# Layer boundaries of an fp32 two-block transformer kernel run in token halves, with scaled tiles in PSUM

## What is computed

```python
    y = jnp.concatenate([y_fox, y_dsa, y_mem], axis=-1)
    y = jnp.einsum('bsn,nd->bsd', y, w_out)
    return layer_norm(ALPHA * x + y, ln_gain, ln_bias)
...
    h = jnp.einsum('bsd,dn->bsn', x, w_in)          # next layer, on the normalised rows
...
    a = rms_norm(h, g_mix_pre[l])                   # second block, on those of layer 2
    proj = a @ w_in[l]
```

## Time and profile before

| | us |
|---|---|
| median of 3 runs | 2196.77 (2196.4 to 2198.25) |
| profiled execution, as a run | 2198.66 |
| its span, first to last instruction | 2196.8 |
| TensorE matmuls busy | 2158.5 |
| VectorE / ScalarE / GpSimd busy | 1279.6 / 1101.5 / 401.4 |

### The profile page before, as it was taken

One profiled execution on the slowest core, in us unless ns is written; L12 is line 12 of the kernel. 1 busy time (PEld: TensorE's weight loads), 2 busy tenths in 40 slices (PEclk: granted clock), 3 DMA queues, 4 the chain that ended last, 5 costly groups with the idle time before them and its releaser, 6 DMA issues.

```text
span 2196.8 us, 29512 instructions
## 1 busy us (share of the span) xinstructions
PE 2158.5 (98%) x11798; PEld 1866.0 (85%) x11798; DVE 1279.6 (58%) x1858; ACT 1101.5 (50%) x1526; POOL 401.4 (18%) x176
## 2 busy tenths in 40 slices
PE   8999999999999999999999999999999999999998
PEld 7888888888988888888888888788888888888886
DVE  5544448765566437855577666665655555555556
ACT  4444554554364554545455455646534534544543
POOL 0000333431000334332006876000000000000000
PEclk9999999999999999999999999999999999999999
DMA  8666555655666555565656655545666666666664
GB/s 287 187 184 185 158 146 162 174 163 174 191 184 185 162 154 154 173 173 163 191 167 199 191 175 161 191 139 169 190 193 191 189 194 192 186 194 193 188 193 141
DMA packets 324376, 394.66 MB, mean 180 GB/s; under 512 B 20320, under 2 KB 252384, under 8 KB 323472
## 3 DMA queue, kind: packets, MB, share of 16 engines
...
## 4 chain that ended last, share of the span: by engine, by line
PE 90%; DVE 5%; ACT 3%; issue 2%; DMA 1%; SPq 0%; DVEq 0%; ACTq 0%
PE acc L645 32%; PE acc L660 17%; PE acc L662 12%; PE acc L647 12%; PE acc L648 12%; ACT high L870 1%; PE tb L711 1%; DVE low L477 1%; PE tb L587 1%; PE obank L733 1%; ACT sc L902 1%; PE sbank L757 1%; PE sbank L701 0%; ACT sc L913 0%; DVE yf L1236 0%
## 5 line engine op out<-in xcount | busy, mean ns | idle before, releaser
L870 ACT ACTIVATE high<-raw 128x1024 fp32r<-128x1024 f32 (+1 forms) x729 | 764.5, 1051 | 790.6 <-PE acc L660 199.4
L477 DVE TENSOR_TENSOR low<-raw,high 128x1024 fp32r<-128x1024 f32 (+1 forms) x569 | 710.7, 1250 | 634.0 <-ACT high L870 630.8
L645 PE MATMUL acc<-xhl,high 128*128 128x512 f32 x3200 | 779.9, 394 | 4.1 <-ACT cb L1159 2.2
L645 PEld LDWEIGHTS acc<-xhl,high 128*128 128x128 f32 x3200 | 586.6, 189 | 116.9 <-issue 2.8
L477 POOL TENSOR_TENSOR low<-raw,high 128x1024 fp32r<-128x1024 f32 x160 | 393.8, 2465 | 743.1 <-ACT high L870 743.0
L660 PE MATMUL acc<-xhl,low 128*128 128x256 f32 x3200 | 434.1, 286 | 2.7 <-DVE low L477 1.4
L660 PEld LDWEIGHTS acc<-xhl,low 128*128 128x128 f32 x3200 | 418.1, 192 | 21.1 <-DVE xhl L1654 1.7
L647 PE MATMUL acc<-high,yhl 128*128 128x512 f32 (+1 forms) x1044 | 384.1, 374 | 1.4 <-DVE work L1528 1.4
L648 PE MATMUL acc<-high,yhl 128*128 128x512 f32 (+1 forms) x1044 | 382.4, 373 | 0.0
L662 PE MATMUL acc<-low,yhl 128*128 128x512 f32 (+1 forms) x1044 | 243.3, 374 | 0.4 <-DVE yhl L1630 0.2
L647 PEld LDWEIGHTS acc<-high,yhl 128*128 128x128 f32 x1044 | 196.8, 188 | 35.9 <-DVE work L1528 1.8
...
## 6 DMA issues: line engine op xcount, KB each, us to landing
raw<-in_w_in SPq DMA_DIRECT2D x336, 512.0 KB, 3.7
raw<-in_w_ff SPq DMA_DIRECT2D x256, 512.0 KB, 4.2
raw<-in_w_out SPq DMA_DIRECT2D x91, 512.0 KB, 4.6
raw<-in_w_mem_kv SPq DMA_DIRECT2D x32, 512.0 KB, 4.9
...
x_nat<-in_mem SPq DMA_DIRECT2D x4, 512.0 KB, 7.7
x_nat<-in_x POOLq DMA_DIRECT2D x4, 512.0 KB, 6.7
yf<-in_ln_gain POOLq DMA_DIRECT2D x2, 1024.0 KB, 5.0
```

The lines of the kernel that those rows point to most:

```text
L477: eng.tensor_tensor(part(low, g), part(raw, g), part(high, g).bitcast(F32), ALU.subtract).then_inc(ready, 1)
L645: ins = pe.matmul(acc[:, 2 * (c.acc % 2) + s, :], wh[:, t, at], vhl, start=first, stop=last)
L870: act.activation(part(high, g), part(raw, g), ACT.Copy).then_inc(high_ready, 1)
```

## The change

- The output projection of the two layers has four chunks of 512 columns (`FCOLS`); statistics are taken over 512 columns per call.
- The last four blocks of its last chunk are done for token tile 0 first, then for tile 1 (`edge`). VectorE does residual, statistics, variance and small steps for each tile by itself (`last_residual`, `row_stats`, `row_var`, `row_scale`), and ScalarE one root for each.
- The first four units are normalised, transposed, scaled and split for tile 0 and then for tile 1; the first four blocks of the next projection run for tile 0 and then tile 1. Units 4 to 7 stay whole. The 36 filler matmuls go.
- The scaled tiles lie in the PSUM banks `sbank` and `obank` (`scaled`) and not in `cb`.
- The lows of the next projection's first eight blocks are GpSimd's. Its queue issues the two row transfers between the fourth and the fifth.
- VectorE's list: the second tile's residual comes behind the scaling of unit 1, its statistics and variance behind unit 1's low part, its small steps behind the scaling of unit 2.
- The rest of the diff renumbers semaphore targets.

```diff
-        for n, (col, width) in enumerate(COLS):
+        for n, (col, width) in enumerate(FCOLS):
...
-        stats = vec("stats", 96).rearrange("p (s c k) -> p s c k", s=ST, c=8)
+        stats = vec("stats", 48).rearrange("p (s c k) -> p s c k", s=ST, c=NF)
...
+        def tiles_in(phase, u, s=0):
+
+            return 12 * phase + (4 * s + u + 1 if u < 4 else 8 + u - 3)
+
+        def scaled(u):
+
+            if u >= 4:
+                return (sbank, obank)[u % 2][:, :].rearrange("p (h n) -> p h n", h=2)
+            return (sbank, obank)[u // 2][:, u % 2 * S:u % 2 * S + S].rearrange("p (h n) -> p h n", h=2)
+
+        edges = [(by[("o", l, NF - 1)].blocks[-4:], by[("fv", l + 1, 0) if l + 1 < DEPTH else ("v2", 0)].blocks)
+                 for l in range(DEPTH)]
...
-        pool_blocks = [[LAYER0 + LAYER_SLOTS * l + b for b in range(40, 134) if b % 2] for l in range(DEPTH)]
+        pool_blocks = [[LAYER0 + LAYER_SLOTS * l + b for b in range(40, 134) if b % 2] + edges[l][1]
+                       for l in range(DEPTH)]
...
+                elif k == ("fv", 0, 0):
+                    pe.wait_ge(xt_ready, 8 + first)
+                elif k == ("v2", 0) or k[0] == "fv" and k[2] == 0:
+                    pe.wait_ge(xt_ready, 16 + tiles_in(k[1] - 1 if k[0] == "fv" else 1, first - 1, rows[-1]))
...
-                if c.blocks.index(g) % 2:
+                if c.blocks.index(g) % 2 and rows != (0,):
                     with_low(False)
                     ins = with_high(False, g == c.blocks[-1])
                 else:
                     with_high(g == c.blocks[0], False)
+                    if between:
+                        between()
                     ins = with_low(g == c.blocks[-1])
...
+            def half_transposes(l, s, u):
+
+                pe.wait_ge(norm_ready, norms(l, u, s))
+                t = t_begin(("nT", l, u, s))
+                for dt in range(2):
+                    ins = pe.transpose(t[:, dt * S + s * P:dt * S + s * P + P],
+                                       x[:, s, 256 * u + dt * P:256 * u + dt * P + P], ident)
+                t_end(ins, ("nT", l, u, s))
+
+            def full_transposes(l, u):
+
+                pe.wait_ge(norm_ready, norms(l, u))
+                transpose_unit(("nT", l, u), x, 256 * u)
+
+            def edge(l):
+
+                out, into = edges[l]
+                for g in out:
+                    weight_block(g, (0,))
+                for g in out[:3]:
+                    weight_block(g, (1,))
+                half_transposes(l, 0, 0)
+                weight_block(out[3], (1,))
+                half_transposes(l, 0, 1)
+                weight_block(into[0], (0,))
+                half_transposes(l, 0, 2)
+                half_transposes(l, 0, 3)
+                weight_block(into[1], (0,))
+                weight_block(into[2], (0,))
+                weight_block(into[3], (0,), lambda: half_transposes(l, 1, 0))
+                half_transposes(l, 1, 1)
+                weight_block(into[0], (1,))
+                half_transposes(l, 1, 2)
+                half_transposes(l, 1, 3)
+                weight_block(into[1], (1,))
+                full_transposes(l, 4)
+                weight_block(into[2], (1,))
+                full_transposes(l, 5)
+                weight_block(into[3], (1,))
+                for u in range(4, 8):
+                    if u < 6:
+                        full_transposes(l, u + 2)
+                    weight_block(into[u])
...
-                    if l and b < 6:
-
-                        pe.wait_ge(norm_ready, norms(l - 1, b + 2))
-                        transpose_unit(("nT", l - 1, b + 2), x, 256 * (b + 2))
-                    weight_block(g0 + b)
+                    if (l == 0 or b >= 8) and b < LAYER_SLOTS - 4:
+                        weight_block(g0 + b)
...
-                spin(job_no(l, "dsa", HS - 1), 36)
-                for u in range(2):
-                    pe.wait_ge(norm_ready, norms(l, u))
-                    transpose_unit(("nT", l, u), x, 256 * u)
+                edge(l)
...
                             act.wait_ge(full, no[("idx", l, f)] + 1)
                             act.activation(rel[f % 2][e], bank[:, :], ACT.Relu, scale=IDIM ** -0.5).then_inc(rel_ready, 1)
 
-                def normalise(u, n=1):
-
-                    for s in range(ST):
+                def normalise(u, n, rows):
+
+                    for s in rows:
                         at = x[:, s, 256 * u:256 * (u + n)]
                         ins = act.activation(at, at, ACT.Identity, bias=nmr[:, s:s + 1], scale=rstd[:, s:s + 1])
                     ins.then_inc(norm_ready, 1)
 
-                def affine_high(n):
-                    u = n % 8
-                    act.wait_ge(aff_ready, n + 1)
-                    act.activation(xh[:, 2 * u:2 * u + 2, :], pair(cb[:, u % 4, :]), ACT.Copy).then_inc(hi_ready, 1)
+                def root_half(s, l=l):
+                    act.wait_ge(var_ready, 2 * l + s + 1)
+                    act.activation(std[:, s:s + 1], var[:, s:s + 1], ACT.Sqrt).then_inc(std_ready, 1)
+
+                def affine_high(u, s=0, l=l):
+                    act.wait_ge(aff_ready, tiles_in(l, u, s))
+                    at = slice(s * P, s * P + P) if u < 4 else slice(0, S)
+                    act.activation(xh[:, 2 * u:2 * u + 2, at], scaled(u), ACT.Copy).then_inc(hi_ready, 1)
 
                 slots(round_block, layer_side, g0, LAYER_SLOTS, TURN if l else LEAD)
 
-                last_sides(round_block, layer_side, g0, LAYER_SLOTS)
+                last_sides(round_block, layer_side, g0, LAYER_SLOTS, 0)
                 nxt = g0 + LAYER_SLOTS
-                root(l + 1)
+                root_half(0)
+                round_block(nxt)
+                act.wait_ge(nmr_ready, 2 * l + 1)
+                normalise(0, 1, (0,))
+                normalise(1, 1, (0,))
+                round_block(nxt + 1)
+                affine_high(0, 0)
+                normalise(2, 2, (0,))
+                affine_high(1, 0)
+                round_block(nxt + 2)
+                root_half(1)
+                affine_high(2, 0)
                 round_block(nxt + 3)
-                act.wait_ge(nmr_ready, l + 1)
-                normalise(0)
-                normalise(1)
-                normalise(2, 2)
-                for u in range(8):
-                    affine_high(8 * l + u)
-                    if u in (0, 2):
-                        normalise(u + 4, 2)
-                    if u >= 2:
-                        round_block(nxt + 2 + u)
+                affine_high(3, 0)
+                act.wait_ge(nmr_ready, 2 * l + 2)
+                normalise(0, 1, (1,))
+                normalise(1, 1, (1,))
+                affine_high(0, 1)
+                normalise(2, 2, (1,))
+                affine_high(1, 1)
+                normalise(4, 2, (0, 1))
+                affine_high(2, 1)
+                affine_high(3, 1)
+                round_block(nxt + 4)
+                affine_high(4)
+                normalise(6, 2, (0, 1))
+                for u in range(5, 8):
+                    round_block(nxt + u)
+                    affine_high(u)
+                round_block(nxt + 8)
+                round_block(nxt + 9)
...
+                def row_stats(n, s):
+                    last[0] = step(dve.bn_stats(stats[:, s, n, :], x[:, s, CW * n:CW * n + CW]))
+
                 def add_residual(n, l=l):
                     c = by[("o", l, n)]
-                    col, width = COLS[n]
-                    at = x[:, :, col:col + width]
+                    at = x[:, :, CW * n:CW * n + CW]
                     acc_done(c)
                     dve.scalar_tensor_tensor(out=at, in0=at, scalar=ALPHA, in1=accs(c), op0=ALU.mult,
                                              op1=ALU.add).then_inc(sum_ready, 1)
                     dve.wait_ge(sum_ready, sums("o", l, n))
 
-                    for c0 in range(0, width, 256):
-                        for s in range(ST):
-                            last[0] = step(dve.bn_stats(stats[:, s, (col + c0) // 256, :], at[:, s, c0:c0 + 256]))
+                    for s in range(ST):
+                        row_stats(n, s)
+
+                def last_residual(s, l=l):
+
+                    n = NF - 1
+                    c = by[("o", l, n)]
+                    at = x[:, s, CW * n:CW * n + CW]
+                    if s:
+                        acc_done(c)
+                    else:
+                        dve.wait_ge(rows_half, l + 1)
+                    ins = dve.scalar_tensor_tensor(out=at, in0=at, scalar=ALPHA, in1=accs(c)[:, s, :], op0=ALU.mult,
+                                                   op1=ALU.add)
+                    if s:
+                        ins.then_inc(sum_ready, 1)
+                        dve.wait_ge(sum_ready, sums("o", l, n))
+                    else:
+                        link(ins)
+
+                def row_var(s):
+
```

(92 more changed lines are left out.)

60 lines of the change are left out of this document (28 added, 32 removed).

## The result

The changed kernel takes 2201.4 us (median; 2199.4 to 2202.8), the kernel before 2198.2 us in the same series: a ratio of 1.0014, 95% interval 1.0008 to 1.0020, so some 3 us slower, where 2.8 us faster was forecast; it lies outside the stated range of 2188.5 to 2199. Its profiled execution has a span of 2200.0 us against 2196.8.

A forecast was written before the change was run, and what follows sets the result against it. TensorE's waits were taken to bound the kernel: first boundary 7.1 - 6.0 + 1.2 = 2.3 us, second 2.3 - 1.6 = 0.7, together 3.0. Less 0.2 for restarts, 2.8 us saved gives 2194.0 us, range 2188.5 to 2199.

The forecast's parts named there:

- Bound and frame: TensorE, busy 2158.5 of 2196.8 us, bounds the kernel; a chain across engines loses 7.1 us at each layer boundary.
- Part 1: Output projection's last chunk 512 wide instead of two of 256: 1.2 us saved per layer, 2.4 us in the kernel.
- Part 2: Boundary done in token halves: without GpSimd interference, 4.2 us of TensorE waits against 7.1, so 2.9 us saved.
- the two smaller waits: TensorE's boundary waits for the second half's first unit, 1.1 us, and ScalarE's last normalisation, 1.0 us.
- Part 3: GpSimd's low halves at the boundary hold VectorE's second-half variance step; the third block's wait becomes 3.5 us instead of 1.6.
- rival (b): At the boundary only the variance step escapes GpSimd's hold, small steps are held: waits 7.4 us, total 2196.6; chance 0.17.
- rival (d): The clock falls at the boundaries without filler matmuls: 4 us each, 2202 us; chance 0.05 together with the rest.
- Part 4: Behind the second boundary VectorE's lows of blocks 8 and 9 come later: TensorE's 1.44 us wait becomes 3.0, costing 1.6.
- Part 5: Row transfers issued behind GpSimd's block 3 land at 23, against 36 when the first residual step asks: cost nothing.
- Slow first matmuls behind waits: First matmul after a wait starts some 0.1 us later, for four more boundary waits: -0.2 us.

The follow-up runs named there:

- last step freed: Changed kernel, but GpSimd begins the next projection's fourth low half only after VectorE's last small step of the second half; 2194.7 us against 2198.4 for the kernel before.
- short GpSimd instructions: Changed kernel with work left out: GpSimd's lows of the next projection's first four blocks cover 32 of 512 columns; 2191.7 us against 2198.4 for the kernel before.
- single-tensor steps: Changed kernel with small steps written as operations of one tensor and a per-partition scalar; 2193.0 us against 2198.5 for the kernel before.
- the version with all moves but the last: Changed kernel with single-tensor small steps, two residual steps and squares one block later, second-half transposes and last normalisation earlier; 2189.9 us against 2198.5 for the kernel before.
- two residual steps later: Changed kernel with two of four residual steps behind the second boundary, and ScalarE's squares of them, one block later; 2202.0 us against 2198.5 for the kernel before.

## Why the prediction was wrong, step by step

- **Bound and frame: right.** In what the change touches, TensorE's waits and what follows from them moved the time, and the chain released by VectorE's xhl was the one to look at.
- **Part 1: right.** The output stage is 1.3 and 1.4 us shorter with the wide chunk alone, 2.4 in all forecast. Alone it gives most of that back, because it lengthens the norm.
- **Part 2: right.** With GpSimd out of the way the third block's wait was 1.18 us for 1.6; the two smaller waits were 1.06 and 0.9 for 1.1 and 1.0.
- **Part 3: the hold was right, the instruction it fell on was wrong.** Taken was that the variance step, because it goes from SBUF to SBUF, is held to 10.55 and the small steps then fit before GpSimd's fourth instruction. The rows show the course of rival (b), which had a chance of 0.17: variance at once, the square held to 10.50, the last step 0.04 us behind the start of GpSimd's next instruction and held to 13.2. The wait was 4.12 us, where the forecast had 3.5 and rival (b) 4.8, a small matter: the boundary's waits are 0.15 + 4.12 + 1.06 + 0.89 = 6.2 us, forecast 6.0. (That the forecast's terms add up to 6.1 is rounding: its own times, 12.7 less 9.3, give 3.4.) The condition quoted for (b) from "What auto-detection actually checks" is only half of what the section says, which also admits equal dimensions; what settles it here is the row, 0.15 us beside a running GpSimd instruction.
- **The step that failed: the sum puts the clock at nothing.** Taking out the fillers has no term in it; the fall of the clock stands only as rival (d), in a part of 0.05. The reason given was that the clock had stayed full from 1116.6 to 1120.71, over three short units, and this was taken to cover a wait of 3.5 us. But in that stretch TensorE never stands still for longer than 0.76 us, and 4.48 us of fillers lie ahead of it:

```profile
1117.03 0.66 PE L587 MATMUL tb<-consts,x_nat 128*128 128x128 f32 x4 [0.44 <-ACT x_nat L1055]
...
1119.42 0.66 PE L587 MATMUL tb<-consts,x_nat 128*128 128x128 f32 x4 [0.76 <-ACT x_nat L1055]
```

The runs show that a wait of 4.12 us drops the clock, that with 28 fillers in it the clock stays, and that taking the fillers out of the kernel before drops it there. The price named in (d), 4 us at each boundary, was too high; a fall costs 1.6. That (d)'s 2202 us is close to the 2201.4 measured is luck: two falls of 4 us on 2194.0, where there were three of 1.6, and the kernel before took 1.4 us more in this series than the 2196.77 that the forecast started from.
- **Part 4: right in kind, mis-sized.** TensorE waits 1.92 + 0.51 us instead of 1.44: 1.0 us more, not 1.6. What the sum lacked is a third fall of the clock behind it, 1.6 us.
- **Part 5: right.** The row transfers cost nothing that any row shows.

Together: at the two boundaries 2.8 us were to be gained and 3.0 were lost, 5.8 us apart. Three falls of the clock are 4.8, the waits at both boundaries 0.4, Part 4 gives back 0.6. That is 4.6; the remaining 1.2 us, about 0.6 per boundary, are not shown by any run. Slow first matmuls behind waits (0.47 to 0.51 us for 0.39) and half units may be in them, of which the prediction had 0.2.

What stays open: the third fall. The same wait (1.91 to 1.93 us) stands in the changed kernel and in seven of the variants. In the profiled executions the clock fell behind it in the changed kernel and in four variants (last step freed, short GpSimd instructions, single-tensor steps, the version with all moves but the last), and not in three (fillers, tiles in SBUF, two residual steps later). The first row is of the changed kernel, the second of the one with fillers. The wait alone doesn't decide it, and no run here separates what does.

```profile
1158.00:1162.00 4.00, 4.00 (x15) 3.48 (x15) 2.11 (x2) 2.80 (x3) 0.00 (x0) 0.57 0.41 131
```

```profile
1150.00:1165.00 15.00, 13.07 (x74) 11.23 (x73) 12.12 (x19) 10.31 (x16) 0.00 (x0) 1.00 0.60 178
```

This is not peculiar to the place. The wait of 1.96 us near 1470 us, the same in all twelve profiled executions, is followed by a full clock in two of them and by a fall in ten. Nor does the kernel alone decide: 27 executions of the kernel before in one series have a mean granted clock of 0.995 to 0.998, and they take 2201.6 us in the median at 0.995 and 2196.8 at 0.998. In all 20 executions of the changed kernel it is 0.993 to 0.995, 0.994 in the profiled one.
